# A two-block transformer kernel on one Trainium2 core: GpSimd makes the low part of a weight block in four instructions instead of one

## What is computed

```python
for l in range(2):                                   # first block
    proj = rmsnorm(x, norm_mix[l]) @ w_in[l]         # q, k, v, indexer, conv, gates
    y_attn = dsa_attention(...) @ w_attn_out[l]      # keeps the 128 best keys
    y_conv = (cB * short_conv(cC * ch, conv_w[l])) @ w_conv_out[l]
    merged = gates[0] * y_attn + gates[1] * y_conv
    x = x + merged @ w_mix_out[l]
    u = rmsnorm(x, norm_mlp[l])
    x = x + jnp.square(jax.nn.relu(u @ w_mlp_up[l])) @ w_mlp_down[l]
x = rmsnorm(x, norm_final)
h = modulate(rms_norm(x, g_mix), sh_m, sc_m)         # second block, one layer
x = x + gt_m * token_mixer(h, ...)                   # attention and mLSTM
h = modulate(rms_norm(x, g_ffn), sh_f, sc_f)
x = x + gt_f * swiglu(h, w_gate, w_up, w_down)
```

## Time and profile before

| | us |
|---|---|
| median of 3 runs | 2361.87 |
| lowest and highest run | 2361.81 and 2367.80 |
| span of the profiled execution, first to last instruction | 2349.5 |
| TensorE busy (matmuls) | 2223.4 |
| VectorE busy | 1111.5 |
| GpSimd busy | 818.4 |
| ScalarE busy | 686.4 |

### The profile page before, as it was taken

One profiled execution on the slowest core, in us unless ns is written; L12 is line 12 of the kernel. 1 busy time (PEld: TensorE's weight loads), 2 busy tenths in 40 slices (PEclk: granted clock), 3 DMA queues, 4 the chain that ended last, 5 costly groups with the idle time before them and its releaser, 6 DMA issues. The chain is left out here.

```text
span 2349.5 us, 26959 instructions
## 1 busy us (share of the span) xinstructions
PE 2223.4 (95%) x10008; PEld 1767.0 (75%) x10008; DVE 1111.5 (47%) x1645; ACT 686.4 (29%) x910; POOL 818.4 (35%) x181
## 2 busy tenths in 40 slices
PE   7998998999999999899999999996999997999998
PEld 5886776877877778677777877875967676878787
DVE  3685325555554637923345455576154344222222
ACT  3123443312212212144332212223254323212121
POOL 3343223434433333332343333332332212433343
PEclk9999999999999999999999999997999988999999
DMA  4322122333333323211223333431211102222222
GB/s 167 98 99 72 54 72 72 108 126 126 127 125 124 108 86 101 90 57 70 72 74 126 139 124 111 143 125 49 90 57 70 54 19 72 92 91 104 90 90 90
DMA packets 35235, 220.98 MB, mean 94 GB/s; under 512 B 5172, under 2 KB 5556, under 8 KB 9400
## 3 DMA queue, kind: packets, MB, share of 16 engines
q1 hardware_dynamic: 27696, 189.80, 23.2%
q10 hardware_dynamic: 7432, 29.74, 3.9%
HBM read 214.54 MB, written 2.10 MB: 92 GB/s over the span
## 5 line engine op out<-in xcount | busy, mean ns | idle before, releaser
L302 POOL TENSOR_TENSOR w_lo<-w_raw,w_hi 128x2048 fp32r<-128x2048 f32 x177 | 818.2, 4623 | 1517.4 <-ACT w_hi L728 1517.4
L319 PE MATMUL ps<-a_hi,w_hi 128*128 128x512 f32 (+1 forms) x1600 | 630.1, 394 | 1.8 <-POOL w_lo L302 1.8
L321 PE MATMUL ps<-a_hi,w_lo 128*128 128x512 f32 (+1 forms) x1600 | 623.2, 390 | 0.0
L320 PE MATMUL ps<-a_lo,w_hi 128*128 128x512 f32 (+1 forms) x1600 | 623.2, 390 | 0.0
L728 ACT ACTIVATE w_hi<-w_raw 128x2048 fp32r<-128x2048 f32 x177 | 339.1, 1916 | 877.3 <-PE ps L321 851.0
L319 PE MATMUL ps<-b_hi,w_hi 128*128 128x512 f32 x816 | 332.3, 407 | 38.4 <-DVE b_lo L1022 26.7
L319 PEld LDWEIGHTS ps<-a_hi,w_hi 128*128 128x128 f32 (+1 forms) x1600 | 297.1, 186 | 87.3 <-issue 21.9
L321 PEld LDWEIGHTS ps<-a_hi,w_lo 128*128 128x128 f32 (+1 forms) x1600 | 297.1, 186 | 66.9
L320 PEld LDWEIGHTS ps<-a_lo,w_hi 128*128 128x128 f32 (+1 forms) x1600 | 297.3, 186 | 63.4 <-issue 0.5
L320 PE MATMUL ps<-b_lo,w_hi 128*128 128x512 f32 x816 | 327.5, 401 | 0.0
L321 PE MATMUL ps<-b_hi,w_lo 128*128 128x512 f32 x816 | 327.1, 401 | 0.0
(11 more groups left out here) (236 smaller groups left out, 2260.0 us busy)
## 6 DMA issues: line engine op xcount, KB each, us to landing
w_raw<-in_weights SPq DMA_DIRECT2D x177, 1024.0 KB, 4.8
v<-in_ada ACTq DMA_DIRECT2D x24, 1024.0 KB, 4.8
x<-in_x_in SPq DMA_DIRECT2D x2, 1024.0 KB, 11.1
out<-x SPq DMA_DIRECT2D x8, 256.0 KB, 2.0
bias<-in_mult_bias ACTq DMA_DIRECT2D x1, 640.0 KB
cs_rope<-in_rope ACTq DMA_DIRECT2D x1, 512.0 KB, 8.3
g<-q ACTq DMA_DIRECT2D x16, 32.0 KB, 2.2
g<-k ACTq DMA_DIRECT2D x16, 32.0 KB, 2.0
```

What stands on the lines that cost most here:

```text
L302: nc.gpsimd.tensor_tensor(w_lo[:, s, :], w_raw[:, s, :], f32(w_hi[:, s, :]), ALU.subtract).then_inc(w_lo_ready, 1)
L319: nc.tensor.matmul(o, wh, hi(kt), start=kt == 0, stop=False)
L320: nc.tensor.matmul(o, wh, lo(kt), start=False, stop=False)
L321: last = nc.tensor.matmul(o, wl, hi(kt), start=False, stop=kt == depth - 1)
```

## The change

GpSimd's one subtraction of 2048 columns becomes four of 512 columns, one after the other. `w_lo_ready` is raised once, by the last of them. Nothing else is changed.

```diff
             def split(n, s):
                 pool.wait_ge(w_hi_ready, n + 1)
-                nc.gpsimd.tensor_tensor(w_lo[:, s, :], w_raw[:, s, :], f32(w_hi[:, s, :]), ALU.subtract
-                                        ).then_inc(w_lo_ready, 1)
+                for c in range(0, BLK, BLK // 4):
+                    piece = slice(c, c + BLK // 4)
+                    last = nc.gpsimd.tensor_tensor(w_lo[:, s, piece], w_raw[:, s, piece], f32(w_hi[:, s, piece]), ALU.subtract)
+                last.then_inc(w_lo_ready, 1)
```

## The result

The changed kernel takes 2297.74 us as the median of four runs (2293.53 to 2298.41); the kernel before took 2364.19 in the same comparison. The ratio is 0.9731, with a 95% interval of 0.9701 to 0.9761. The forecast was 2311.1 us, range 2298 to 2342, faster. It was added up from 2361.87, the kernel before's median of three runs; 2364.19 is its median of four. The direction is right, and the gain, 64 to 66 us, is larger than the 50.8 forecast.

A forecast was written before the change was run, and what follows sets the result against it. TensorE, busy 95%, was taken as the bound, so gains come where it stands still or its clock falls. 26.2 + 10.6 + 6.6 + 2.3 + 6.1 - 1.0 = 50.8 us off 2361.9 gives 2311.1 us, range 2298 to 2342.

The forecast's parts named there:

- GpSimd keeps what it holds across the four pieces: Rival: VectorE may never get in between pieces, so all stalls stay; about 2365 us, chance 0.15.
- VectorE getting in one piece late: Rival: VectorE gets in, but one piece later than forecast; about 2327 us, chance 0.11.
- slower: Rival: pieces cost more than GpSimd's slack, a fixed cost of 1 us or more; about 2412 us, chance 0.05.
- chunk boundaries: Eleven places where TensorE waits 26.7 us for `b_lo`; only 0.5 us stays at the last, gain 26.2 us.
- convolution, twice: Convolution to `w_conv_out`, once per layer: VectorE's shorter stalls let TensorE resume 5.3 us earlier, gain 10.6 us.
- merge, twice: The last `b_lo` stall in each merge ends near 384.3 instead of 387.6; gain 3.3 us each, 6.6 us.
- norm before the last MLP: Second norm of the last block: stalled addition ends 3.2 us earlier, 0.9 given back; gain 2.3 us.
- start of the last block: A like stall before TensorE's 8.2 us wait gives nothing, since dense two-input VectorE additions stand behind it.
- `w_lo` and `a_lo` late elsewhere: Where TensorE waits for `w_lo`, at block 1 (+0.2) and 1932.9 (+0.75), pieces make it later; loss 1.0 us.
- clock: TensorE's half-clock stretches after two merges and last two boundaries: 3.3 us back plus half of 5.6, 6.1 us.
- The price of a piece: On GpSimd, three more instructions per block cost 0.1 to 0.3 us, taken as 0.2, mostly hidden by slack.
- The 12.4 us between span and median: Profiled span 2349.5 us against the runs' median 2361.87 for the kernel before; the difference was left as it is.

The follow-up runs named there:

- the last group: Kernel before again (2361.97 us), and against it eight pieces again (0.9716), a 256/512 mix (0.9728) and thirty-two pieces of 64 columns (1.0289).
- the second traces of the two kernels: Repeats with no new edit: kernel before again, 2361.97 us, ratio 1.0000; change itself (four pieces) again, 2295.26 us, ratio 0.9720 against the kernel before.

## Why the prediction was right, and where it was off

The mechanism is shown: GpSimd and VectorE exclude each other for the length of one instruction, when both read SBUF in the way these do, and the other gets its turn at the end of each piece. The rival that GpSimd keeps what it holds across the four pieces is out by the 1.37 and 1.74 us above; so is VectorE getting in one piece late, and "slower" needed thirty-two pieces. Term by term, with the waits of TensorE in the two traces:

| term | forecast, us | measured, us |
|---|---|---|
| chunk boundaries | 26.2 | 26.7 to 0.4: 26.3 |
| convolution, twice | 10.6 | 19.8 to 12.0: 7.8 |
| merge, twice | 6.6 | 11.7 to 1.8, but `w_lo` +2.4: 7.5 |
| norm before the last MLP | 2.3 | 7.1 to 3.9, next 2.2 to 2.9: 2.5 |
| start of the last block | 0 | 8.2 to 5.9, next 3.7 to 5.7: 0.3 |
| loop branch | not seen | 2.9 to 0.2: 2.7 |
| `w_lo` and `a_lo` late elsewhere | -1.0 | 3.7 to 4.2, 13.0 to 13.7: -1.2 |
| clock | 6.1 | 12.1 |
| sum | 50.8 | 58.0, span 57.8 |

The waits were forecast to fall by 44.7 us and fell by 45.9. That this is so close is in part luck: the 2.7 us at the loop branch, which nobody foresaw, stand against the 2.8 us missing at the convolution.

**The convolution walk was too kind.** It is on the clock of the kernel before. The changed kernel runs 2.63 us later here (ScalarE starts the same two splits at 143.94 and 176.66, not at 141.31 and 174.03), so 2.63 is to be taken off its times. The walk had VectorE's `y_lo` start at 186.8, before GpSimd's turn, and the last take end at 188.3. They came at 190.16 - 2.63 = 187.5 and 189.5. The timeline of VectorE in the changed kernel, in the stretch where pieces and VectorE alternate:

```profile
180.58 1.35 DVE L1143 TENSOR_SCALAR g<-g,lp 128x512 f32<-128x512 f32 x1
182.00 3.32 DVE L1146 SCALAR_TENSOR_TENSOR g<-g,lp 128x511 f32<-128x511 f32 x2
185.47 0.69 DVE L1024 TENSOR_TENSOR g<-ps,rms 128x512 f32<-128x512 f32 x1
186.25 0.69 DVE L1024 TENSOR_TENSOR g<-g 128x512 f32<-128x512 f32 x1
```

The multiplication with one SBUF tensor (L1143) takes 1.35 us; all eight of the kernel before took 0.49, and none of them started inside an instruction of GpSimd. I had let only instructions with two SBUF tensors wait. It is a tensor times a value per partition. The Trainium skill, SBUF — State Buffer, "Who interferes with whom", counts `tensor_scalar` among those that can use both ports and then contend with GpSimd; this row agrees with it. Each of the two products behind it took 1.62 us as well. Of the 3.3 us that VectorE was ahead, the pieces so took 2.6 back where the walk had 1.8. GpSimd's next turn had also come forward by 0.7 us, to 189.49 - 2.63 = 186.86; `y_lo` met it and took 1.14 us instead of 0.69. Together that is 1.2 us, and the gap fell to 5.0 us instead of 3.6.

**The price of a piece was too low.** Forecast: 0.2 us for three more instructions. Measured: 0.17 us for each by the minima, 0.14 by the distance of their starts (1219 ns for 512 columns, 680 for 256), so some 0.45 us a block, and `w_lo` takes 5.04 us as a median instead of 4.61. Its sum is 932 us, over the 870 I had named, which also holds the pieces' waits for VectorE; and the mean of `b_lo` is 0.99 us, not 0.8. It mattered little, since the slack of the earlier trace rows took it. At the start of the merge TensorE now waits 1.2 us for `w_lo`, once per layer; there most of the delay is VectorE's turns (`w_lo` takes 6.38 us, against 5.04 alone), which the prediction had as 2 us but charged nothing for.

**The clock gave twice the term.** I took only the stretches behind four gaps, and half of the two at the merges. In the profiled execution all four are gone, which is the full 8.9 us. Two more went: at 785.1 (6.49 us of matmuls at a granted clock of 0.50) and at 809.0 behind the loop branch (3.16 us), by the same halving 3.2 and 1.6 us. A new one near 29 costs about 1.5. Those at the convolution shrank from 10.2 to 6.8 us, but TensorE is busy 4.3 and 4.4 us in the first of them before and after, so that gave nothing. Part of this is not steady. The mean granted clock of the kernel before lay between 0.969 and 0.974 over the 29 runs of the last group, that of four pieces between 0.981 and 0.985 over nine. Between the second traces of the two kernels the matmul time falls by 24.4 us (2229.1 to 2204.7), not 12.1, while the time in which TensorE stands still falls by 47.6, as before (45.7).

**The 12.4 us between span and median was misread.** I carried it as a fixed part. In the changed kernel it is 1.8 us (2293.53 against 2291.7), and the runs of the kernel before show the same 1.8. The other 10 us are scatter: the profiled execution was one of the kernel's fastest, with the clock at 0.974, and most others were at 0.969 to 0.972 and 2360 to 2367 us. That is why the medians differ by 64 to 67 us where the traces differ by 57.8. With the clock term that was too small, it is also why the result lies at the low edge of the range, 0.3 us below it.

## What to carry to other kernels

When an elementwise instruction of VectorE has a median as expected and a maximum longer by about the length of a GpSimd instruction (0.69 and 4.69 us here), suspect that the two exclude each other, and look at single instances. If they do, the fix is a shorter instruction on the engine that has slack, sized so that the first end comes before the waiting one is needed. It pays where one instruction waits alone; where VectorE is dense, the same GpSimd time is only served in portions. Price the split against the slack: here four to sixteen pieces came out much alike, sixteen with 22.5 us of new waits that other gains outweighed, and thirty-two were slower than none.

## What the runs showed of the hardware that I had not expected

**A weight load may stand before the fetch of instructions.** At the end of the first layer TensorE's loop branch (L441) took 6.5 and 6.4 us in the two traces of the kernel before, and TensorE idled 2.9 us; in every changed kernel it took 3.3 to 3.9 us. The loads of `w_raw` start when `w_lo` is ready. The issue of that load before, and after:

```profile
801.77 0.33 SPq L288 DMA_DIRECT2D w_raw<-in_weights  x1
```
```profile
782.68 0.33 SPq L288 DMA_DIRECT2D w_raw<-in_weights  x1
```

The branch begins at 802.29 before and at 782.16 after. So the load is issued 0.52 us ahead of it in the one and 0.52 us behind it in the other. In the packets of the trace, those of the load begin 0.44 us after the branch before, and the first packet of instructions comes 4.1 us after it, when the load is through. After, that packet goes at 1.0 us and the load begins at 1.5. With only odd blocks split the load is issued 2.9 us ahead, is almost through in time, and the packet goes at 1.3 us. With two pieces it is issued 0.06 us ahead, its packets begin at 0.9, and the packet of instructions still goes at 1.3 us, so being a little ahead is not enough. If the order is the cause, the longer `w_lo` moved the load out of the way by accident. That it explains the 2.7 us is argued from these positions; no run moved the load alone.

**A fixed cost per GpSimd instruction of 0.14 to 0.17 us**, beside 2.11 ns a column, holds from 1024 down to 64 columns; the tiny fills of the earlier trace rows, 0.03 us apart, do not tell it.

**The two engines took turns one for one.** In the merge of the changed kernel VectorE's instructions at 370.21, 371.32, 373.79 and 374.72 last 1.18, 1.78, 1.01 and 1.75 us, one for each of GpSimd's four pieces, and `w_lo` takes 6.38 us from 369.55. Neither engine got in twice in a row there while the other waited.
